# Summing down-projection weights with adding DMAs in DRAM instead of with VectorE

## The reference

```
xn = rms_norm(x); z = xn @ w_in          # q, k, v (8 heads x 64), conv h, B, C (512 channels)
attn = three dilated sliding-window branches merged by their softmax denominators
conv = B * conv3(C * h)
h = x + concat(attn, conv) @ w_out
hn = rms_norm(h)
y = rms_norm(h + (silu(hn @ w_gate) * (hn @ w_up)) @ w_down)     # w_down: 2816 x 1024
```

## Time and profile before

| | us |
|---|---|
| median of 3 runs (lowest, highest) | 1215.83 (1215.45, 1215.98) |
| the profiled execution | 1217.06 |
| its span | 1215.3 |
| TensorE busy | 1197.9 |
| VectorE busy | 679.3 |
| GpSimd busy | 509.6 |
| ScalarE busy | 438.1 |

### The profile page before, as it was taken

The page is one execution under the profiler, slowest core; times in us unless marked ns, Lnnn a source line. Parts: engine busy times, 40 slices in busy tenths (PEclk is TensorE's granted clock), DMA queues, the critical chain, the costliest instruction groups (busy, mean ns, idle before and its releaser), DMA issues.

```text
span 1215.3 us, 22908 instructions
## 1 busy us (share of the span) xinstructions
PE 1197.9 (99%) x9257; PEld 1136.5 (94%) x9257; DVE 679.3 (56%) x1133; ACT 438.1 (36%) x828; POOL 509.6 (42%) x420
## 2 busy tenths in 40 slices
PE   7999999999999999999999999999999999999998
PEld 6998779889877799999999999999999999999998
DVE  6888214414677623479555444454554178756665
ACT  7111120000378711355443343334333443445452
POOL 3436023233144341052788768776878640000020
PEclk9999999999999999999999999999999999999999
DMA  5478676343223151012614342245444995323223
GB/s 214 156 281 262 230 262 235 139 174 103 84 92 111 48 185 65 1 45 69 241 48 170 116 149 96 106 175 218 166 173 163 345 342 203 94 88 96 86 74 108
DMA packets 70393, 182.66 MB, mean 150 GB/s; under 512 B 7376, under 2 KB 24464, under 8 KB 66320
## 3 DMA queue, kind: packets, MB, share of 16 engines
q1 hardware_dynamic: 70144, 180.92, 42.5%
q10 hardware_dynamic: 144, 0.27, 0.1%
HBM read 136.33 MB, written 44.83 MB: 149 GB/s over the span
## 4 chain that ended last, share of the span: by engine, by line
PE 48%; DVE 2%; POOL 1%; issue 1%; DMA 0%; ACT 0%; DVEq 0%; ACTq 0%
PE ps L1577 9%; PE ps L1579 9%; PE ps L1578 9%; PE ps L1626 6%; PE ps L1627 6%; PE ps L1628 6%; PE ps L1601 1%; PE ps L1600 1%; PE ps L1602 1%; POOL w_lo L966 1%; DVE norms L2735 1%; DMA w_stage<-in_w 0%; DVE combo_b L2262 0%; POOL w_stage L1009 0%; DVE w_lo L2663 0%
## 5 line engine op out<-in xcount | busy, mean ns | idle before, releaser
L1118 PE MATMUL ps<-act_hi,w_hi 128*128 128x352 f32 x480 | 157.4, 328 | 8.2 <-DVE act_lo L2267 8.2
L1577 PE MATMUL ps<-combo,w_hi 128*128 128x264 f32 x544 | 154.9, 285 | 1.7 <-DVE evac L2651 1.2
L1120 PE MATMUL ps<-act_hi,w_lo 128*128 128x352 f32 x480 | 154.8, 323 | 0.0
L1119 PE MATMUL ps<-act_lo,w_hi 128*128 128x352 f32 x480 | 154.7, 322 | 0.0
L1579 PE MATMUL ps<-combo,w_lo 128*128 128x264 f32 x544 | 154.5, 284 | 0.0
L1578 PE MATMUL ps<-combo,w_hi 128*128 128x264 f32 x544 | 154.3, 284 | 0.0
L1626 PE MATMUL ps<-hid,w_hi 128*128 128x264 f32 x536 | 152.7, 285 | 0.0
L1627 PE MATMUL ps<-hid,w_hi 128*128 128x264 f32 x536 | 152.4, 284 | 0.0
L1628 PE MATMUL ps<-hid,w_lo 128*128 128x264 f32 x536 | 152.3, 284 | 0.0
L966 POOL TENSOR_TENSOR w_lo<-w_stage,w_hi 128x512 fp32r<-128x512 f32 (+1 forms) x51 | 76.2, 1495 | 106.1 <-ACT w_hi L1704 106.0
L1577 PEld LDWEIGHTS ps<-combo,w_hi 128*128 128x128 f32 x544 | 102.2, 188 | 2.1 <-issue 1.4
(11 more groups left out here) (470 smaller groups left out, 3237.1 us busy)
## 6 DMA issues: line engine op xcount, KB each, us to landing
w_stage<-in_w SPq DMA_DIRECT2D x56, 512.0 KB, 4.1
resid<-in_state_k SPq DMA_DIRECT2D x8, 1792.0 KB, 11.0
norms<-in_w SPq DMA_DIRECT2D x22, 512.0 KB, 4.4
t_d<-norms SPq DMA_DIRECT2D x11, 1024.0 KB, 4.9
h_d<-evac SPq DMA_DIRECT2D x36, 264.0 KB, 2.3
v_buf<-in_state_v SPq DMA_DIRECT2D x9, 1024.0 KB, 7.0
resid<-in_xT SPq DMA_DIRECT2D x16, 528.0 KB, 7.3
late<-h_d SPq DMA_DIRECT2D x6, 1056.0 KB, 12.9
```

What stands on the lines that cost most here:

```text
L1118: pe.matmul(out, hi, rhs_hi, start=first, stop=False)
L1119: pe.matmul(out, hi, rhs_lo, start=False, stop=False)
L1120: return pe.matmul(out, lo, rhs_hi, start=False, stop=last)
L1577: pe.matmul(out, hi[:, wk], x_hi[:, k, tk], start=(k == 0 and first), stop=False, skip_group_check=not first)
```

## The change

The sums of w_down's blocks are made in DRAM. ScalarE issues two DRAM-to-DRAM copies that put block (0,0) into the slot of P5 in `t_d` and block (0,1) into that of P7. GpSimd issues adding DMAs (`accum_op=ALU.add`), each of them on up to three of the eleven steps, [128, 3, 512] words: eight during the conv units, behind `straight(16)` to `straight(23)`, which add block (0,1) to P5 and block (1,1) to P7. SyncE then copies P5's sums to the slots of P6 and P4. GpSimd adds block (1,1) to both in eight more DMAs between the last out-projection units, waits for all, and adds block (1,0) to P4 in four more. The sums have only plus signs; so the signs of three activation sums and of three products' additions to the residual change. The loads, subtractions and stores in the feed-forward go, and with them the waits of SyncE and ScalarE for the last store.

```diff
+        def down_blocks(x, y):
+            return w[DOWN0 + HK * x:DOWN0 + HK * x + HK].rearrange("k p n -> p k n")[:, :, 512 * y:512 * y + 512]
+        def sums_blocks(product):
+            return t_d.rearrange("k p n -> p k n")[:, :, 512 * W_SUMS[product]:512 * W_SUMS[product] + 512]
...
 # SyncE, behind load_second(3) and unit(28)
+            sp.wait_ge(sums_added, 16 * 8)
+            for product in ("P6", "P4"):
+                sp.dma_start(sums_blocks(product), sums_blocks("P5")).then_inc(sums_copied, 16)
...
-            def load_sums(k):
-                if k:
-                    sp.wait_ge(scratch_out, 16 * (KT + k))
-                else:
-                    sp.wait_ge(dve_lo, FIRST_PARTS + 4)
-                for x in range(2):
-                    sp.dma_start(sums_buf[:, 1024 * x:1024 * x + 1024], w[DOWN0 + HK * x + k]).then_inc(sums_in, 16)
-            def store_sums(k):
-                sp.wait_ge(w_sums, 3 * k + 3)
-                sp.dma_start(t_d[k], sums_buf).then_inc(scratch_out, 16)
...
 # SyncE, ahead of the down loads
-            sp.wait_ge(scratch_out, 16 * (KT + HK))
+            sp.wait_ge(sums_added, 16 * 20)
...
 # GpSimd
+            def add_block(product, x, y, part):
+                ks = slice(3 * part, min(3 * part + 3, HK))
+                pool.dma_start(sums_blocks(product)[:, ks, :], down_blocks(x, y)[:, ks, :], accum_op=ALU.add
+                               ).then_inc(sums_added, 16)
             for u in range(3, OUT0):
                 straight(u)
                 if u >= CONV0 + 5 and (u - CONV0 - 5) % 3 == 0:
                     conv_low((u - CONV0 - 5) // 3)
+                if u == CONV0 + 4:
+                    pool.wait_ge(sums_copied, 32)
+                if u >= CONV0 + 4:
+                    add_block(*(("P5", 0, 1) if u % 2 else ("P7", 1, 1)), (u - CONV0 - 4) // 2)
...
             pool.wait_ge(pv_done, STEPS // 2)
-            for u in range(OUT0 + 3, FFN0):
-                straight(u)
+            straight(OUT0 + 3)
+            straight(OUT0 + 4)
+            pool.wait_ge(sums_copied, 64)
+            for part in range(4):
+                add_block("P4", 1, 1, part)
+                add_block("P6", 1, 1, part)
+                if part < FFN0 - OUT0 - 5:
+                    straight(OUT0 + 5 + part)
+            pool.wait_ge(sums_added, 16 * 16)
+            for part in range(4):
+                add_block("P4", 1, 0, part)
             weight_low(0, "G")
...
 # ScalarE
             sample_exp(0)
             sample_turned(0)
+            act.dma_start(sums_blocks("P5"), down_blocks(0, 0)).then_inc(sums_copied, 16)
+            act.dma_start(sums_blocks("P7"), down_blocks(0, 1)).then_inc(sums_copied, 16)
             conv_high(0)
...
-                if s == 0:
-                    act.wait_ge(scratch_out, 16 * (KT + HK))
...
 # VectorE: first_down_sums and second_down_sums and their calls go
-                dve.tensor_tensor(first, halves[:, :, 1, :], first, ALU.subtract).then_inc(w_sums, 1)
-                dve.tensor_tensor(w22, w22, w11, ALU.subtract).then_inc(w_sums, 1)
-                dve.tensor_tensor(w21, w21, w22, ALU.subtract).then_inc(w_sums, 1)
...
-                dve.tensor_tensor(s1, a21, a22, ALU.add).then_inc(act_sums, 1)
+                dve.tensor_tensor(s1, a22, a21, ALU.subtract).then_inc(act_sums, 1)
...
-                dve.tensor_tensor(a11, s1, a11, ALU.subtract).then_inc(act_sums, 1)
+                dve.scalar_tensor_tensor(a11, s1, -1.0, a11, ALU.mult, ALU.subtract).then_inc(act_sums, 1)
...
-                dve.tensor_tensor(place(HOME["s1"][k]), place(HOME["a12"][k]), place(HOME["a11"][k]), ALU.subtract
-                                  ).then_inc(act_sums, 1)
+                dve.scalar_tensor_tensor(place(HOME["s1"][k]), place(HOME["a12"][k]), -1.0, place(HOME["a11"][k]), ALU.mult,
+                                         ALU.subtract).then_inc(act_sums, 1)
...
-                dve.tensor_tensor(out, two_banks(2 * m), out, ALU.add).then_inc(down_put, 1)
+                dve.tensor_tensor(out, out, two_banks(2 * m), ALU.subtract if DOWN_PRODUCTS[i] in MINUS else ALU.add
+                                  ).then_inc(down_put, 1)
...
+MINUS = ["P5", "P3", "P7"]
```

More of the change, by code:

```diff
@@ L303, in build @@
         h_out = [[sem(f"h_out{h}{i}") for i in range(2)] for h in range(2)]
-        sums_in, scratch_out = sem("sums_in"), sem("scratch_out")
+        sums_copied, sums_added, scratch_out = sem("sums_copied"), sem("sums_added"), sem("scratch_out")
         part_in_a = {n: [sem(f"{n}_in{i}") for i in range(3)] for n in ("a11", "a12", "a21", "a22")}
@@ L348, in build @@
             sem(n) for n in ("t_made", "gate1", "gate2", "up2", "hidden1", "hidden2", "dve_lo"))
-        w_sums, act_sums, down_low, down_put = sem("w_sums"), sem("act_sums"), sem("down_low"), sem("down_put")
+        act_sums, down_low, down_put = sem("act_sums"), sem("down_low"), sem("down_put")
         last_ss = sem("last_ss")
@@ L764, in _ @@
                 n = a + 2
-                sums, done = DOWN_SUMS[a], DOWN_SUMS.get(a - 2, ())
                 store_hidden(0, a - 1)
                 store_hidden(1, a - 1)
[L768 to L773, removed]
                 load_raw(*(("gate", n) if n < PAIR_END else ("up", n)))
                 load_raw(*(("up", n) if n < PAIR_END else ("gate", n)))
[L776 to L780, removed]
                 if n < PAIR_END:
@@ L2761, in block_low @@
                 dve.tensor_tensor(which[1], block_f[(2, 1, 0, 2)[n]], f32(which[0]), ALU.subtract).then_inc(dve_lo, 1)
[L2763 to L2772, removed]
-                dve.tensor_tensor(first, halves[:, :, 1, :], first, ALU.subtract).then_inc(w_sums, 1)
-            def second_down_sums(k):
-                w11, w12, w21, w22 = weight_quarters(k)
-                dve.wait_ge(w_sums, 3 * k + 1)
-                dve.tensor_tensor(w22, w22, w11, ALU.subtract).then_inc(w_sums, 1)
-                dve.wait_ge(w_sums, 3 * k + 2)
-                dve.tensor_tensor(w21, w21, w22, ALU.subtract).then_inc(w_sums, 1)
             def hidden_sums(k):
@@ L2956, in _ @@
                 b, n = a + 1, a + 2
-                sums = DOWN_SUMS[a]
                 put_sub(a, "p1")
@@ L2961, in _ @@
                 put_sub(a, "p7")
-                if sums and a > PAIR_FIRST:
-                    first_down_sums(sums[0])
                 put_sub(a, "p5")
                 put_sub(a, "p4")
-                if sums and a > PAIR_FIRST:
-                    second_down_sums(sums[0])
                 put_sub(a, "p3")
@@ L2976, in _ @@
                 second_up(b)
-                if len(sums) > 1:
-                    first_down_sums(sums[1])
-                elif n < PAIR_END:
+                if n < PAIR_END:
                     pair_t_sums(n + 1)
@@ L2982, in _ @@
                 first_hidden(b)
-                if len(sums) > 1:
-                    if n < PAIR_END:
-                        pair_t_sums(n + 1)
-                    second_down_sums(sums[1])
-                if a == PAIR_FIRST:
-                    first_down_sums(0)
-                    second_down_sums(0)
             for f in range(PAIR_END, FT):
@@ L3127 @@
 BLOCK_SUMS, FIRST_PARTS = 8, 32
-DOWN_SUMS = {4: (0,), 6: (), 8: (1,), 10: (2,), 12: (3, 4), 14: (5, 6), 16: (7, 8), 18: (9, 10)}
 POS, GATE_NO, HI_NO, LO_NO, GATE_AT, SUB_AT = {}, {}, {}, {}, {}, {}
```

2 lines of the change are left out of this document (removed).

## The result

The changed kernel has a median of 1235.51 us over four runs (1232.36 to 1237.09) beside 1215.90 for the kernel before on the same chips: ratio 1.0157, interval 1.0136 to 1.0179. It is slower by 19.6 us, where 6.4 were forecast. The profiled execution took 1236.06 us, span 1234.3, which is 19.0 us more than before.

A forecast was written before the change was run, and what follows sets the result against it. TensorE's matrix products were taken to bound the kernel. Terms 0 (removed) + 0 (swapped) + 6.4 (convolution) + 0 (out-projection) gave +6.4 us: 1223.5 profiled, 1222.2 as median; range 1215 to 1239.

The forecast's parts named there:

- The bound: Whole kernel: TensorE's own 9257 matrix products set the end; other engines' work counts only where it makes TensorE wait.
- What is removed and changed in place, 0: Feed-forward and down phase: dropped subtractions, loads and stores, and swapped VectorE operations, are hidden behind TensorE; priced 0.
- Rival (d): Middle stretches: VectorE's relief shows, at most 0.9 plus 2.9 us of TensorE idle, 1212.0 at best; chance 0.04.
- The convolution, +6.4: Convolution: GpSimd's wait for ScalarE's copies delays unit 17's split and a cached-value block; TensorE waits 6.4 us; chance 0.36.
- The smaller wait near 181: Convolution: the second pair of value blocks lands late beside the copies; 1.5 us, adding nothing to the sum.
- Out-projection, +0: Between out-projection and feed-forward: GpSimd's adds finish before the first feed-forward weights, at 3.8 to 6.4 us each; priced 0.
- Rival (c): Before the feed-forward: an add costs over 7.2 us, so first weights are late; at 10 us each, 1246; chance 0.09.
- The copies of SyncE and the residual loads, 0: Attention and out-projection: SyncE's two copies take 18.7 us and delay residual loads 0.4 us, within 10 us slack; priced 0.
- The clock: Whole kernel: no term for a lower clock; TensorE's busy time was said not to change.

The follow-up runs named there:

- e1: The changed kernel without the DRAM copies, the twenty adding DMAs and their waits, plain weight blocks loaded instead of sums: 1215.81 us, ratio 0.9993.
- e7: The changed kernel with 40 extra thrown-away TensorE products ahead of the wait for the feed-forward's first weights: 1231.79 us, ratio 1.0122.
- e2: The changed kernel with GpSimd's last four adds moved from ahead of the feed-forward to behind its last down-phase splits: 1222.21 us, ratio 1.0044.

## Why the prediction was wrong

**The bound.** Right. TensorE sets the end, and only lateness counts; both new losses are waits of TensorE.

**What is removed and changed in place, 0.** Right: e1 has both and measures 0.9993 (0.9983 to 1.0002) of before. Rival (d) could have been worth 3.8 us at best, and nothing of it is told from the scatter.

**The convolution, +6.4.** Right in mechanism and nearly in size. Copies in by 209.6 (212 said), the block issued at 215.46 (217.6 said), landed 7.8 us later (7.7 said), a wait of 3.9 us (6.4 said). The earliness of 2 us is most of the difference. It comes from the start: the copies were issued from 168.31, where the data were priced to flow from 170.8, and the 41.3 us from there to 209.6 are the 41.2 that had been forecast. That the whole came out so well is in part luck, as its parts don't stand: the same two copies on SyncE took 23.2 us, where 18.7 was the price alone; if ScalarE's needed as much, the loads beside them took 18.1 us and not the 22.5 that were left for them. The place cost 5.8 us by the trace, more than its wait, because the lower clock after the wait was in no term. The smaller wait near 181 did not come. The first add's issue took 1.46 us (1.0 said). ScalarE's second issue lasted 8.54 us, which its idle covered.

The Trainium skill's 214 GB/s for copies inside HBM (page "DMA: Bandwidth & Descriptors", section "Latency and other measured facts"), which the prediction cited, is too low here: SyncE's two copies, issued at 413.63 and 414.32, landed after 14.4 and 22.5 us, so both were in 23.2 us after the first issue, 5.77 MB / 23.2 us = 249 GB/s, with residual loads beside them from 431.90 on.

**Out-projection, +0.** This step failed: "An add's data takes 3.8 us if reading sets the pace, 3.8 + 2.6 = 6.4 us if the write follows. ... Both bounds are below it; price 0, but narrowly". The frame was right, as it worked out a limit of 7.2 us each for eleven adds in a row. The size was not: 8.26 us each, and by the prediction's own formula 11 x 8.26 - 79.7 = 11.2 us, against 9.1 us of waiting. Both bounds were bandwidths, bytes divided by a rate. What was missing was the part of an add that doesn't go with its bytes, some 3.3 us by the half-wide adds; the bytes' own part, 5.0 us by the same estimate, lies inside the bounds. An add took 7.9 us (median of all twenty) to land, beside 3.8 to 6.4 priced, and the next issue came only behind the landing. Rival (c), with 9 in 100, came true beside the forecast and not in its stead; that the two could happen together was not priced. The wait's 9.1 us then brought 3.7 us more by the clock (e7), and the two together were worth 13.3 (e2). The measured time lies in the stated range of 1215 to 1239 only because its upper end had been left open for a long wait in the convolution, which did not come; the range had left rival (c) out.

**The copies of SyncE and the residual loads, 0.** Right: TensorE waits for none of them, though the copies took 23.2 us and not 18.7.

**The clock.** In no term; the prediction said that TensorE's busy time should not change, and it rose by 5.6 us. After 9.1 us of idle the granted clock was 0.50, and 0.74 on average over 540 to 560; after 3.9 us it was 0.79 over 8 us. The Trainium skill, page "TensorE: Matmul & The Clock Gate", Part 1, says that the array's lower clock is its idle state and that activity lifts it; the traces agree, 0.50 beside 1.00, and e7 shows the activity side.

## What to carry to other kernels

A DMA issued from GpSimd is no free errand: price its engine as held from one large adding DMA to the landing of the one ahead, and ask what else is queued on that engine; cutting an add into smaller ones did not help, 1262.69 and 1243.34 us beside 1235.51. Here splits of weights were, and the cure was to issue the adds where nothing follows them. Bound an unknown transfer by a fixed part too, not only by bytes over a rate, and where a price of nothing hangs on such a bound by a tenth, treat the other side as just as likely. For every wait of TensorE that you predict, add the slow products behind it: here about 4 us for 9 us of idle.

## What the runs showed of the hardware

- Adding DMAs, DRAM to DRAM, 384 rows of 2 KB, issued one behind the other: 8.1 us from issue to issue, the next about 0.3 us behind the landing; half as wide 6.0 us; plain ones land after 5.6 us (median), and some go out two at a time.
- GpSimd's held issues fall where the running count of rows would pass a turn of some 1008 to 1055 places (an estimate; the kernels ask for 1024), two places for an adding row, one for a plain one, 16 for an issue.
- An adding row is one packet, a plain one half a packet, and the adding queue takes 7.6% of the DMA engines' time for what plain copies do in 3.4%.
- Issuing from GpSimd takes 1.2 us for an add of 384 rows, 0.8 us for one of 128, 0.7 us for a plain copy of 384.
- Of ScalarE's two copies of 1408 rows each the first issue took 0.67 us, the second 8.54; SyncE's two took 0.65 and 0.69 us. Why the one differs is open.
